# A hybrid SSM, attention and feed-forward layer: sums of squares by VectorE, maxima moved ahead, dt columns in column groups

## The reference, cut to what matters

```python
hn = rms_norm(x, g_pre_mix)
z, xbc, dt_raw, q, k, v = jnp.split(hn @ w_in, IN_SPLITS, axis=-1)   # dt_raw: 8 of 3080 columns
dt = jax.nn.softplus(dt_raw.astype(f32) + dt_bias.astype(f32))
...
p = jax.nn.softmax(jnp.where(visible, s, -jnp.inf), axis=-1)         # s: (2 per head, 4 heads)
att = p[:, :, 0] - lam * p[:, :, 1]
o = jnp.einsum('bhqk,bkhe->bqhe', att, v)
...
f = (jax.nn.silu(hn @ w_gate) * (hn @ w_up)) @ w_down
h = h + rms_norm(f, g_post_ffn)                                      # the last norm
```

## Time and profile before

| what | value |
|---|---|
| median of 3 runs | 1964.87 us (1963.97 to 1968.98) |
| profiled execution, its own time | 1961.18 us |
| span in its trace | 1959.4 us |
| TensorE matmuls busy | 94% of the span |
| VectorE, ScalarE, GpSimd busy | 48%, 28%, 22% |
| mean granted TensorE clock | 0.98 of full speed |

### The profile page before, as it was taken

The page is one execution under the profiler, slowest core; times in us unless marked ns, Lnnn a source line. Parts: engine busy times, 40 slices in busy tenths (PEclk is TensorE's granted clock), DMA queues, the critical chain, the costliest instruction groups (busy, mean ns, idle before and its releaser), DMA issues.

```text
span 1959.4 us, 28792 instructions
## 1 busy us (share of the span) xinstructions
PE 1837.7 (94%) x11950; PEld 1770.3 (90%) x11950; DVE 932.9 (48%) x1605; ACT 542.2 (28%) x1165; POOL 431.7 (22%) x211
## 2 busy tenths in 40 slices
PE   7999989999778898989899999999999999999996
PEld 7998979998677798977799899999999999999995
DVE  6853167575777538225536634233234233233246
ACT  6433212332765435114424610100100100100024
POOL 0000001113000032310232035314323333243133
PEclk9999999999899999999999999999999999999998
DMA  5143222222112421124311211101111111021032
GB/s 201 65 138 116 91 83 77 87 71 83 59 44 92 147 80 44 65 106 159 134 39 62 95 43 54 52 24 44 48 39 43 34 54 44 22 65 43 22 118 97
DMA packets 61966, 146.21 MB, mean 75 GB/s; under 512 B 4368, under 2 KB 34448, under 8 KB 60304
## 3 DMA queue, kind: packets, MB, share of 16 engines
q1 hardware_dynamic: 38736, 110.35, 16.5%
q10 hardware_dynamic: 23104, 34.06, 5.1%
HBM read 120.95 MB, written 23.44 MB: 74 GB/s over the span
## 4 chain that ended last, share of the span: by engine, by line
PE 78%; DVE 12%; ACT 5%; issue 4%; DMA 1%; SPq 1%; POOL 0%; ACTq 0%; POOLq 0%; DVEq 0%
PE bank L199 23%; PE bank L203 23%; PE bank L202 23%; PE bank L1128 2%; DVE at_sm L2123 1%; DVE NL L278 1%; DVE hid_l L2432 1%; DMA w_raw<-in_wall 1%; PE bank L764 1%; DVE acc L1893 1%; PE bank L823 1%; ACT E L1518 1%; PE bank L264 1%; DVE H L366 1%; DVE ATT L2140 1%
## 5 line engine op out<-in xcount | busy, mean ns | idle before, releaser
L202 PE MATMUL bank<-NL,w_hi 128*128 128x384 f32 x1800 | 608.4, 338 | 0.0
L199 PE MATMUL bank<-NH,w_hi 128*128 128x384 f32 x1608 | 547.7, 341 | 5.2 <-DVE xp L1870 2.8
L203 PE MATMUL bank<-NH,w_lo 128*128 128x384 f32 x1608 | 542.7, 338 | 0.0
L602 POOL TENSOR_TENSOR w_hi<-w_raw,one 128x1024 fp32r<-128x1024 f32 x82 | 159.9, 1950 | 929.9 <-PE bank L199 835.3
L202 PEld LDWEIGHTS bank<-NL,w_hi 128*128 128x128 f32 x1800 | 340.9, 189 | 2.3 <-issue 0.9
L199 PEld LDWEIGHTS bank<-NH,w_hi 128*128 128x128 f32 x1608 | 304.4, 189 | 7.8 <-issue 6.6
L203 PEld LDWEIGHTS bank<-NH,w_lo 128*128 128x128 f32 x1608 | 304.1, 189 | 0.0
L604 POOL TENSOR_TENSOR w_lo<-w_raw,w_hi 128x1024 fp32r<-128x1024 f32 x90 | 228.5, 2539 | 105.7 <-ACT w_hi L329 99.3
L2415 DVE TENSOR_TENSOR ACC<-ACC,bank 128x384 f32<-128x384 f32 x240 | 132.1, 554 | 119.7 <-PE bank L203 119.7
L199 PE MATMUL bank<-hid_h,w_hi 128*128 128x384 f32 x528 | 181.0, 343 | 5.9 <-DVE ACC L2415 5.2
L203 PE MATMUL bank<-hid_h,w_lo 128*128 128x384 f32 x528 | 177.4, 336 | 0.0
(11 more groups left out here) (354 smaller groups left out, 2783.0 us busy)
## 6 DMA issues: line engine op xcount, KB each, us to landing
w_raw<-in_wall SPq DMA_DIRECT2D x130, 512.0 KB, 3.3
cK<-in_cmk SPq DMA_DIRECT2D x8, 1024.0 KB, 7.3
cV<-in_cmv SPq DMA_DIRECT2D x8, 1024.0 KB, 4.9
H<-in_xT SPq DMA_DIRECT2D x5, 1536.0 KB, 12.3
scratch_h<-H ACTq DMA_DIRECT2D x3, 1536.0 KB, 6.0
Hback<-scratch_h ACTq DMA_DIRECT2D x3, 1536.0 KB, 10.6
Kb<-in_kc SPq DMA_DIRECT2D x8, 512.0 KB, 4.2
Vb<-in_vc SPq DMA_DIRECT2D x8, 512.0 KB, 5.0
```

The lines of the kernel that those rows point to most:

```text
L199: m = mm(out, ah, bh, start=(i == 0), stop=False)
L202: mm(out, ah, bl, start=False, stop=False)
L203: m = mm(out, al, bh, start=False, stop=(i == n - 1))
L602: pool.tensor_tensor(whi[s][:], raw[s % 2][:], bc(one[:, 0:1], [P, WI]), ALU.mult).then_inc(w_hi, 1)
```

## The change

1. Last norm. For chunks 0 and 1 the squares of the four pairs go to `sq1` and `sq0`, VectorE adds them (`last_add`, three adds of 128x768 a chunk), and TensorE sums once (`whole_sum`). Chunk 2 keeps its four pieces. VectorE's `last_norm` of chunk 0 stands behind units 18 to 21 instead of 15 to 18, and chunk 2 has a count of its own, so that VectorE no longer waits for GpSimd. The store of the first half of chunk 2 is issued ahead of that of the second half of chunk 1.
2. Attention, from u = 16 on. `maxes(u + 1)` stands directly behind `probs(u)`. `o_copy` is at h = 0 and ScalarE's `o_norm` at h = 2.
3. dt. The weights are padded from 8 to 32 columns and not split. Feature tiles 2j and 2j + 1 go to column group j, that is to PSUM partitions 32j to 32j + 31, as plain fp32 products; 16 of them for each chunk. `dtr` has 128 rows, and nine plain products with a matrix of zeros and ones (`C_SEL`) add the four groups and transpose.

```diff
@@ dt columns, TensorE
-            pe.wait_ge(s_wdt, 1)
+            pe.wait_ge(ld["wdt"], 16)
             for c in range(CH):
                 pe.wait_ge(xb_ev, xb_no[6, c] + 1)
-                three(B[c][0:SH, 0:NC],
-                      [(g("wdh")[:, k, :], g("wdl")[:, k, :], g("NH")[:, c, k, :], g("NL")[:, c, k, :])
-                       for k in range(KT)]).then_inc(s_dtm, 1)
+                for k in range(2):
+                    for x in ("NH", "NL"):
+                        for j in range(4):
+                            m = mm(B[c][rows_of(j), 0:NC], g("wdr")[:, 2 * j + k, :], g(x)[:, c, 2 * j + k, :].bitcast(F32),
+                                   start=(k == 0 and x == "NH"), stop=(k == 1 and x == "NL"))
+                m.then_inc(s_dtm, 1)
...
                     for t in range(NT):
-                        m = nc.tensor.transpose(B[3][:, SH * t:SH * t + SH], g("dtr")[0:SH, tok(t)], ident[0:SH, 0:SH])
+                        m = mm(B[3][:, SH * t:SH * t + SH], g("dtr")[:, tok(t)], cst[:, C_SEL:C_SEL + SH], start=True,
+                               stop=True)
@@ dt columns, ScalarE and VectorE
-            act_f(g("wdh")[:], g("wdr")[:], ACT.Copy).then_inc(s_dtu, 1)
...
-                act_f(g("dtr")[0:SH, cs(c)], B[c][0:SH, 0:NC], ACT.Copy).then_inc(s_dtc, 1)
+                act_f(g("dtr")[:, cs(c)], B[c][:, 0:NC], ACT.Copy).then_inc(s_dtc, 1)
...
-            TT(g("wdl")[:], g("wdr")[:], g("wdh")[:].bitcast(F32), ALU.subtract).then_inc(s_wdt, 1)
@@ attention, ScalarE
-                if h == 1 and t:
+                if t and h == (2 if u >= UH else 1):
                     o_norm(t - 1)
@@ attention, VectorE
                 probs(u)
+                if u >= UH:
+                    for v in coming(u):
+                        maxes(v)
+                    if h == 0:
+                        o_copy(t - 1)
                 if h in (1, 2) and t + 2 < NT - 1:
...
-                if h == 1 and t:
+                if h == 1 and 0 < t < UH // H:
                     o_copy(t - 1)
                 if h == 3 and t:
                     o_scale(t - 1)
-                for v in coming(u):
-                    maxes(v)
+                if u < UH:
+                    for v in coming(u):
+                        maxes(v)
@@ last norm, TensorE
+        def whole_sum(pe, p):
+            pe.wait_ge(n_std, p)
+            mm(B[7][:, 0:NC], ones[:, :], g("rsl")[:, cs(p - P_END)], start=True, stop=False)
+            pe.wait_ge(n_sum, 28 + 3 * (p - P_END) + 3)
+            for k in range(2):
+                m = mm(B[7][:, 0:NC], ones[:, :], g("sq1")[:, k, :], start=False, stop=(k == 1))
+            m.then_inc(n_pc, 4)
...
-                if q >= 5 and q % 2:
-                    sum_piece(pe, P_END + (q - 5) // KT, (q - 5) % KT // 2, NC)
+                if q in (12, 20):
+                    whole_sum(pe, P_END + (q - 12) // KT)
+                if q >= 21 and q % 2:
+                    sum_piece(pe, P_END + 2, (q - 21) // 2, NC)
@@ last norm, VectorE
+        def last_add(dve, p, i):
+            dve.wait_ge(n_sq, 4 * p + i + 1)
+            if i > 1:
+                dve.wait_ge(n_sum, 28 + 3 * (p - P_END) + i - 1)
+            TT(g("sq1")[:], g("sq1")[:], g("sq0")[:], ALU.add).then_inc(n_sum, 1)
...
-                    dve.wait_ge(p_t, 2 * CH + i + 1)
-                    dve.wait_ge(n_res, 4 * CH + 4 * (CH - 1))
+                    dve.wait_ge(p_t, 2 * CH + 8 + 2 * (i - 8) + 1)
                     dve.wait_ge(ld["Hb0"], 16 * CH)
-                    TT(hb, hb, a, ALU.add).then_inc(n_res, 1)
+                    TT(hb, hb, a, ALU.add).then_inc(p_t, 1)
...
-                if q in (15, 16, 17, 18, 22):
-                    last_norm((15, 16, 17, 18, 22).index(q))
-            for i in range(5, 4 * CH):
+                if q in (5, 7, 9, 13, 15, 17):
+                    last_add(dve, P_END + (q - 5) // KT, (q - 5) % KT // 2 + 1)
+                if q in (18, 19, 20, 21):
+                    last_norm(q - 18)
+            for i in range(4, 4 * CH):
                 last_norm(i)
@@ stores, SyncE
-            for i, n in ((0, 2), (2, 2), (4, 2), (6, 2), (8, 2), (10, 1), (11, 1)):
+            for i, n in ((0, 2), (2, 2), (4, 2), (8, 2), (6, 2), (10, 1), (11, 1)):
```

More of the change, by code:

```diff
@@ L37 @@
 C_C0, C_C1 = 1096, 1097
-C_END = 1098
+C_SEL = 1098
+C_END = 1106
 G_MEM, G_PREMIX, G_POSTMIX, G_PREX, G_POSTX, G_PREF, G_POSTF = (8 * i for i in range(7))
@@ L258, in sum_piece @@
             pe.wait_ge(n_sq, 4 * p + i + 1)
-            if p and i == 0:
+            if i == 0:
                 pe.wait_ge(n_std, p)
-            if i == 0:
                 mm(B[7][:, 0:w], ones[:, :], g("rsl")[:, cs(p - P_END)], start=True, stop=False)
@@ L265, in sum_piece, with last_square @@
             m.then_inc(n_pc, 1)
+        def whole_sum(pe, p):
[5 more added lines that the diff above has]
+            m.then_inc(n_pc, 4)
+        def last_square(act, p, i, src):
+            n = 28 + 3 * (p - P_END)
+            if i == 0:
+                act.wait_ge(n_sum, n)
+                act.wait_ge(n_pc, 4 * P_END)
+            elif i == 1:
+                act.wait_ge(n_pc, 4 * p)
+            elif p < P_END + CH - 1:
+                act.wait_ge(n_sum, n + i - 1)
+            else:
+                act.wait_ge(n_pc, 4 * p + i - 1)
+            s = g("sq1" if i == 1 or (i == 3 and p == P_END + CH - 1) else "sq0")
+            act_f(s[:], src[:, 2 * i:2 * i + 2, :], ACT.Square).then_inc(n_sq, 1)
+        def last_add(dve, p, i):
[3 more added lines that the diff above has]
+            TT(g("sq1")[:], g("sq1")[:], g("sq0")[:], ALU.add).then_inc(n_sum, 1)
         def h_high(act, p, z, half, gain):
@@ L585, in _ @@
             weights(I_WX + 2, N_ITEMS)
-            for i, n in ((0, 2), (2, 2), (4, 2), (6, 2), (8, 2), (10, 1), (11, 1)):
+            for i, n in ((0, 2), (2, 2), (4, 2), (8, 2), (6, 2), (10, 1), (11, 1)):
                 c, k = i // 4, slice(i % 4 * 2, i % 4 * 2 + 2 * n)
-                sp.wait_ge(n_res, 4 * CH + i + n)
+                if c < CH - 1:
+                    sp.wait_ge(n_res, 4 * CH + i + n)
+                else:
+                    sp.wait_ge(p_t, 2 * CH + 8 + 2 * (i - 8 + n))
                 sp.dma_start(y_o[:, k, cs(c)], g("Hback")[:, k, cs(c)]).then_inc(y_out, 16)
@@ L1382, in _ @@
                     act_f(D6[:, :, 1], D6[:, :, 0], ACT.Abs).then_inc(s_dtu, 1)
+                    act.wait_ge(s_dtu, 3)
+                    act_f(D6[:, :, 2], D6[:, :, 1], ACT.Exp, scale=-1.0).then_inc(s_dtu, 1)
                     act.wait_ge(s_dtu, 4)
-                    act_f(D6[:, :, 2], D6[:, :, 1], ACT.Exp, scale=-1.0).then_inc(s_dtu, 1)
-                    act.wait_ge(s_dtu, 5)
                     act_f(D6[:, :, 3], D6[:, :, 2], ACT.Ln, bias=1.0).then_inc(s_dtu, 1)
@@ L1811, in _ @@
                     act.wait_ge(f_de, 2 + 24 * (NG - 1) + KT * c + 2 * i + 2)
-                    pre_sq(act, P_END + c, i, y, NC)
+                    last_square(act, P_END + c, i, y)
                     act.wait_ge(n_sq, 4 * (P_END + c) + i + 1)
@@ L1911, in _ @@
             conv(1)
-            dve.wait_ge(s_dtu, 1)
-            TT(g("wdl")[:], g("wdr")[:], g("wdh")[:].bitcast(F32), ALU.subtract).then_inc(s_wdt, 1)
             for n in range(2, I_TM):
@@ L1932, in _ @@
             TT(u0, u0, bc(row[:, R_DTB:R_DTB + SH].unsqueeze(1), [P, NT, SH]), ALU.add).then_inc(s_dt, 1)
-            dve.wait_ge(s_dtu, 3)
+            dve.wait_ge(s_dtu, 2)
             link(TT(nlam[:], row[:, R_LAM + 1:R_LAM + 2], row[:, R_LAM:R_LAM + 1], ALU.subtract))
@@ L1940, in _ @@
             link(TS(vec[:, V_SUB:V_SUB + 1], vec[:, V_SUB:V_SUB + 1], 0.8, None, ALU.mult))
-            dve.wait_ge(s_dtu, 6)
+            dve.wait_ge(s_dtu, 5)
             u, e, ln = D6[:, :, 0], D6[:, :, 2], D6[:, :, 3]
@@ L2480, in _consts @@
     c[:, C_BB:C_BB + DB] = p[:, None] // DS == np.arange(DB)
+    c[:, C_SEL:C_SEL + SH] = p[:, None] % 32 == np.arange(SH)
     c[:, C_C1] = p // DS % 2
@@ L2538 @@
         "wall": wall,
-        "wdt": wi[:, 1536:1544].reshape(KT, P, 8).transpose(1, 0, 2),
+        "wdt": np.pad(wi[:, 1536:1544].reshape(KT, P, 8).transpose(1, 0, 2), ((0, 0), (0, 0), (0, 24))),
         "consts": _consts(),
```

6 lines of the change are left out of this document (2 added, 4 removed).

## The result

| | before | after |
|---|---|---|
| median of 4 runs | 1965.97 us (1963.97 to 1968.98) | 1945.95 us (1940.04 to 1947.99) |
| profiled execution, its own time | 1961.18 us | 1944.58 us |
| span in its trace | 1959.4 us | 1942.8 us |

The ratio of the runs is 0.9899 with a 95% interval of 0.9881 to 0.9916: 19.9 us (16.5 to 23.4) faster. The forecast was 9.2 us and its range ended at 1951.0 us, so the change gives about twice what was forecast.

A forecast was written before the change was run, and what follows sets the result against it. TensorE was taken to set the pace nearly everywhere, other engines only at open handovers. Savings of 2.7 (dt), 5.0 (attention) and 1.5 us (last norm) sum to 9.2 us: 1964.87 becomes 1955.7 us, range 1951.0 to 1961.0.

The forecast's parts named there:

- The sum: Whole kernel: dt 2.7, attention 5.0 and last norm 1.5 us together save 9.2 us; no other stage counted.
- What bounds the kernel now: Opening step: TensorE, busy 94% of the span, sets the pace nearly everywhere, other engines only where a handover stands open.
- dt columns: dt stage on TensorE: 48 plain fp32 products replace 72; with the nine sums and small terms, 2.7 us saved.
- The round: dt columns: one round of four column groups takes 0.68 us; twelve plus 0.2 for entering and leaving make 8.4 us.
- The sums: dt columns: nine plain products replace the transposes and take 2.2 us, 1.5 us more than before.
- The rule quoted against the change: dt columns: a weight load overlaps running products only when its row group differs, so the groups' loads would add up.
- rival 2: dt columns: weight loads aren't hidden, 11.3 us, saving 1.2 instead of 4.1; 1958.6 us in all; chance 0.06.
- Rival 3: dt columns: column groups don't run at once, 30.7 us in place of 12.5; 13.2 us slower, 1978.1 us; chance 0.05.
- Attention: Attention from query tile 4 on: each pitch between maxima comes down to the undisturbed one, saving 5.0 us (3 to 6).
- Rivals 1 and 4: 1: attention gives back half, 1958.2 us, chance 0.13. 4: nothing arrives in dt or attention, 1964.9 us, chance 0.04.
- Last norm: End of the program: earlier squares and no GpSimd gap of 3.10 us, last stores binding, save 1.5 us (0 to 2.9).
- its base: Whole kernel: the median before the change, 1964.87 us, from which the 9.2 us were taken.

The follow-up runs named there:

- e4: Kernel before with the constants 8 unread columns wider and nothing else: 1957.05 us, ratio 0.9974.
- e5: Kernel before with the dt part alone, constants at their old width, ones read from the padding of the dt weights: 1959.71 us, ratio 0.9981.
- e2: Kernel before with the attention part alone: 1959.24 us, ratio 0.9983.
- e6: Changed kernel without its dt part (attention and last norm alone): 1953.91 us, ratio 0.9965 to the kernel before.
- c1: Changed kernel run again, unchanged: 1946.28 us, ratio 0.9919 to the kernel before.
- g3: Changed kernel run a third time, unchanged: 1946.90 us, ratio 0.9910 to the kernel before.
- c0: Kernel before, unchanged, built and run again as control: 1962.20 us, ratio 1.0000.
- g2: Kernel before with a 96-byte unused tile in front and constants 8 columns wider (weights +96 bytes, rest +128): 1958.47 us, ratio 0.9958.
- h1: Kernel before with the constants array 8 columns wider in the chip's memory only, its SBUF tile as before: 1962.26 us, ratio 0.9996.
- e9: Kernel before with the constants 16 columns wider, tiles behind moved by 64 bytes, split weights not: 1961.86 us, ratio 0.9997.

## Why the prediction was wrong

- **The sum, the step that failed.** It added three places and let every other stage keep its time. Widening the constants was part of the change and got no term at all. It is worth 4 to 5 us in the feed-forward stage: 818.5 to 822.3 us in the seven traces with the tiles at their old place, 815.8 to 817.2 in the three of the changed kernel, and 5.1 us (2.9 to 7.3) by e4's times. "What bounds the kernel now" had called TensorE busy and stopped there. The windows of the kernel before, read for the number of products and not for the busy share, would have shown two rates at one clock.
- **dt columns, a term mis-sized.** 2.7 us forecast, 3.5 measured (e5: 3.7). The round was taken at 0.68 us plus 0.2 for the ends; it is 0.645, the time of one such product alone (0.64 in the prediction), so the four groups run wholly side by side. The sums took 2.07 us for 2.2. The rule quoted against the change ("TensorE: Matmul & The Clock Gate", packing small matmuls, the Trainium skill), worked out as rival 2 at 11.3 us, doesn't hold here: the twelve rounds took 7.88 us. Rival 3 fell with it.
- **Attention, right.** 5.0 forecast and 5.0 in the trace, 4.9 to 5.0 in e2, e6, c1 and g3 against c0. The mechanism is the one foretold: the pitches of t = 5 are 4.4 to 4.6 us. Rivals 1 and 4 fell.
- **Last norm, right.** 1.5 forecast, 1.4 to 1.9 in the traces. Its steps came within 0.7 us each, the stores bind at the end (SyncE's wait for the last store is 3.8 us, before 2.1), and no gap of 3.10 us is left.
- **Scatter, underrated.** The prediction set its base on three runs, 1964.87 us. In five later comparisons the kernel before had medians of 1962.3 to 1967.6 us. The clock's dip in the state-space stage alone moves an execution by 2 us, and the stage of the samples and projections by 4.

The four terms that have a cause, 3.5 + 5.0 + 1.6 + 4.5 (the last between e4's 5.1 us by time and its 4.0 by trace against c0), make 14.6 us; with the interval of e4's times alone, 13.0 to 17.4. The repeated comparisons gave 15.9 us (13.4 to 18.3) and 17.7 us (14.0 to 21.2), which agree; the first one, 19.9 us (16.5 to 23.4), lies 1.9 us above 14.6 even at its lower end, but within what the last term leaves open. Whether there is a rest stays open. Open too is what about the addresses sets TensorE's pitch: not the place modulo 64, and not the distance to the weights modulo 128. Which of the moved tiles counts was not tried.

## What to carry to other kernels

When a diff changes the size of anything in SBUF, all that is allocated behind it moves, and code that nobody edited can run at another rate; compare the untouched stages first, by products per stretch and not by busy share, before a gain or a loss is put down to the edit. A control that changes only the size (an unread column) costs one run and tells it apart. But look at every stage: the 64 bytes that made one stage some 4 us shorter made another as much longer. And where two engines work on SBUF side by side and slow each other down, one of them alone can be quicker.

## What the runs showed of the hardware

- TensorE, busy 100% of 60 us at a granted clock of 1.00, passed 341 to 348 of the same products of 384 columns. The median distance of two starts was 0.173 us in every stretch of 20 us, in each of the eleven traces with the tiles moved by 32, 64 or 128 bytes in SBUF (g2, with the weights moved by 96, among them), and another in 15 to 32 stretches in each of the nine with 0, 96, or all tiles moved by 32. A wider array in memory without moved tiles left it slow (h1). In the kernel before, two executions had the slower rates in different groups (c0 took 820.8 us, before 819.9).
- Four column groups of plain fp32 products, 128 by 32 weights and 384 columns each, take 0.645 us together, weights included.
- The place of tiles can work against one stage and for another: with 64 bytes more (e9) the state-space stage took 275.5 us, against 271.0 in h1, and the feed-forward stage 816.7, against 820.4.
- One VectorE instruction of 128x768, with two inputs in SBUF, took 0.95 us alone and 2.42 us when it began 0.24 us behind one of GpSimd.
- One and the same program had a stretch of TensorE at the lower clock level in the state-space stage in one execution and not in another: 273.1 and 271.2 us.
